# Two 2048-wide blocks on one core: query and key projection in paired 512-column steps, and three shifts in the slot tables around it

## What is computed

```python
hn = _rmsnorm(h, norm1_g)
q, k, v, u = jnp.split(hn @ w_in, [1024, 2048, 3072], axis=-1)
attn_out = dilated_attention(rope(q), rope(k), v)       # 8 heads of 128
bu = einsum('bsgp,gnp->bsgn', u, b_bar)                 # S5 input, 64 groups x 64 states, complex
_, states = lax.associative_scan(combine, (a_seq, bu))  # along the 256 tokens
y = einsum('bsgn,gpn->bsgp', states, c_mat).real + d_skip * u
```

## Time and profile before

| what | value |
|---|---|
| time, median of 3 runs | 3140.21 us (3140.12 to 3142.82) |
| the profiled execution | 3142.39 us, span 3140.7 us, granted clock 0.997 |
| PE busy | 3087.9 us, 98% of the span |
| DVE busy | 2036.6 us, 65% |
| ACT busy | 1632.1 us, 52% |
| POOL busy | 320.0 us, 10% |

### The profile page before, as it was taken

The page is one execution under the profiler, slowest core; times in us unless marked ns, Lnnn a source line. Parts: engine busy times, 40 slices in busy tenths (PEclk is TensorE's granted clock), DMA queues, the critical chain, the costliest instruction groups (busy, mean ns, idle before and its releaser), DMA issues.

```text
span 3140.7 us, 47334 instructions
## 1 busy us (share of the span) xinstructions
PE 3087.9 (98%) x17098; PEld 2691.0 (86%) x17098; DVE 2036.6 (65%) x2406; ACT 1632.1 (52%) x2088; POOL 320.0 (10%) x313
## 2 busy tenths in 40 slices
PE   8999999999999999999999999999999999999998
PEld 7989878888888888899998887888887888888887
DVE  7998987665566565657766777455555655555555
ACT  5545655654444365658754555445445544444453
POOL 1563440000000000004420000000000000000000
PEclk9999999999999999999999999999999999999999
DMA  8766666666666665555565555566655666666664
GB/s 296 247 224 186 193 184 197 188 189 190 193 187 187 201 188 167 193 185 171 177 189 187 175 165 177 184 195 209 200 184 158 200 191 191 191 189 192 193 188 154
DMA packets 176780, 600.99 MB, mean 191 GB/s; under 512 B 20320, under 2 KB 30688, under 8 KB 175488
## 3 DMA queue, kind: packets, MB, share of 16 engines
q1 hardware_dynamic: 164016, 567.18, 58.1%
q10 hardware_dynamic: 8976, 18.68, 1.6%
q0 software_dynamic: 3648, 13.24, 1.3%
HBM read 588.54 MB, written 10.49 MB: 191 GB/s over the span
## 4 chain that ended last, share of the span: by engine, by line
PE 84%; DVE 10%; issue 2%; ACT 1%; DMA 1%; POOL 1%; ACTq 0%; SPq 0%; DVEq 0%; POOLq 0%
PE gemm_psum L402 39%; PE gemm_psum L450 22%; PE gemm_psum L460 11%; PE gemm_psum L430 8%; DVE weights_lo L1471 3%; DVE late L1630 1%; PE gemm_psum L426 1%; DVE late L1623 1%; ACT weights_hi L876 1%; DVE late L1617 1%; DVE late L1634 1%; DVE late L1624 1%; DVE late L1633 0%; PE bank_s L737 0%; PE bank_s L705 0%
## 5 line engine op out<-in xcount | busy, mean ns | idle before, releaser
L1471 DVE TENSOR_TENSOR weights_lo<-weights,weights_hi 128x1024 fp32r<-128x1024 f32 (+1 forms) x1064 | 1312.4, 1238 | 896.6 <-ACT weights_hi L876 895.3
L876 ACT ACTIVATE weights_hi<-weights 128x1024 fp32r<-128x1024 f32 (+1 forms) x1064 | 1109.2, 1051 | 1113.1 <-PE gemm_psum L402 621.6
L450 PE MATMUL gemm_psum<-x_parts,weights_hi 128*128 128x512 f32 x3008 | 754.0, 392 | 0.7 <-DVE x_parts L2201 0.7
L450 PEld LDWEIGHTS gemm_psum<-x_parts,weights_hi 128*128 128x128 f32 x3008 | 541.6, 189 | 98.2 <-DVE x_parts L2201 0.9
L460 PEld LDWEIGHTS gemm_psum<-x_parts,weights_lo 128*128 128x128 f32 x3008 | 410.3, 190 | 29.3
L460 PE MATMUL gemm_psum<-x_parts,weights_lo 128*128 128x256 f32 x3008 | 419.4, 282 | 0.0
L402 PE MATMUL gemm_psum<-weights_hi,u_hi 128*128 128x512 f32 x1472 | 393.8, 389 | 0.0
L402 PE MATMUL gemm_psum<-weights_lo,u_hi 128*128 128x512 f32 x1472 | 387.4, 385 | 0.2 <-DVE weights_lo L1471 0.2
L402 PE MATMUL gemm_psum<-weights_hi,u_lo 128*128 128x512 f32 x1472 | 387.1, 385 | 0.0
L402 PE MATMUL gemm_psum<-weights_hi,x_parts 128*128 128x512 f32 x1280 | 322.9, 394 | 2.8 <-DVE x_parts L1682 1.9
L402 PEld LDWEIGHTS gemm_psum<-weights_lo,u_hi 128*128 128x128 f32 x1472 | 272.8, 188 | 56.6 <-DVE weights_lo L1471 0.9
(11 more groups left out here) (396 smaller groups left out, 2242.2 us busy)
## 6 DMA issues: line engine op xcount, KB each, us to landing
weights<-in_w_branch SPq DMA_DIRECT2D x192, 512.0 KB, 3.6
weights<-in_w_gu SPq DMA_DIRECT2D x176, 512.0 KB, 3.7
weights<-in_w_up SPq DMA_DIRECT2D x128, 512.0 KB, 4.2
weights<-in_w_down SPq DMA_DIRECT2D x128, 512.0 KB, 4.2
weights<-in_w_dn SPq DMA_DIRECT2D x64, 512.0 KB, 4.2
weights<-in_w_in_qk SPq DMA_DIRECT2D x32, 512.0 KB, 4.8
weights<-in_w_mem_k SPq DMA_DIRECT2D x32, 512.0 KB, 3.9
weights<-in_w_mem_v SPq DMA_DIRECT2D x32, 512.0 KB, 4.0
```

The source lines that it names most:

```text
L450: mm = pe.matmul(GP[:, 2 * p + n, :], HI[:, j % RING, cols], XS[:, (j % UNITS) * g.kt + k, :, :].rearrange("p a t -> p (a t)"), start=firs ...
L876: act.activation(HI[:, j % RING, 0:g.kt * GC], RAW[:, j % RING, 0:g.kt * GC], ACT.Copy)\
L1471: dve.tensor_tensor(LO[:, j % RING, cols], RAW[:, j % RING, cols], HI[:, j % RING, cols].bitcast(f32), ALU.subtract).then_inc(lo_done, 1)
```

## The change

There are four edits.

1. `in_qk` is run by `unit_pairs`. ACT gets a copy of the second halves in slots 3 and 7, and DVE's single multiply of the result by the row norm becomes an add, a wait for it, and a multiply in place.
2. In the first body of `in_qk`, the two `ssm_in` move from slots 2 and 4 to slots 4 and 6 on PE; on DVE the first `rotate_in` moves from slot 0 to 1 and the first scan from slot 2 to 3.
3. The scores of each head move on PE from slot 4 to slot 5.
4. In slot 6 of `mem_k` and `mem_v`, DVE runs the reciprocal before the scan instead of after it.

```diff
             def ssm(slot, b, q0):                              # PE
                 q, half = b.halved().plus(q0), b.c % 2
-                if slot == (2 if isinstance(b(), int) and b() == 0 and q0 == 0 else 0):
+                opening = isinstance(b(), int) and b() == 0 and q0 == 0
+                if slot == (4 if opening else 0):
                     ssm_in(q, 2 * half)
...
-                if slot == 4:
+                if slot == (6 if opening else 4):
                     ssm_in(q, 2 * half + 1)
...
-                if slot == 4:
+                if slot == 5:
                     wait(pe, rope_done, h(1, 1))
...
                     ssm(j, b, 0)
-                    units(in_qk, b, j, x)
+                    unit_pairs(in_qk, b, j, rows_before=False)
...
             def qk_events(slot, b):                            # ACT
                 ssm(slot, b, 0)
+                if slot in (3, 7):
+                    p = slot // 4
+                    wait(act, mm_done, b(SLOTS, SLOTS * in_qk.first + slot + 1))
+                    act.activation(ZP[:, ix(b(4, 8 + 2 * p), 2), :], GP[:, 2 * p:2 * p + 2, T:2 * T], ACT.Copy).then_inc(half_done, 1)
...
             def ssm(slot, b, q0):                              # DVE
                 s = b.times(2).plus(4 * q0)
-                if slot in (0, 4):
+                opening = isinstance(b(), int) and b() == 0 and q0 == 0
+                if slot in ((1, 4) if opening else (0, 4)):
                     rotate_in(s.plus(slot // 4), slot // 4)
-                if slot in (2, 6):
+                if slot in ((3, 6) if opening else (2, 6)):
                     scan_and_rotate_out(s.plus(slot // 4), slot // 4)
...
                 if slot in (3, 7):
-                    scaled_out(in_qk, b, slot, ZP[:, ix(b(4, 8 + 2 * (slot // 4)), 2), :])
+                    p = slot // 4
+                    tiles = ZP[:, ix(b(4, 8 + 2 * p), 2), :]
+                    wait(dve, half_done, b(2, p + 1))
+                    dve.tensor_tensor(tiles, GP[:, 2 * p:2 * p + 2, 0:T], tiles, ALU.add).then_inc(evac[p], 1)
+                    wait(dve, evac[p], b(1, in_qk.evacs + 1))
+                    dve.tensor_tensor(tiles, tiles, row(rms[:, 0, :]), ALU.mult)
...
             def mem_k_events(slot, b):
+                if slot == 6:
+                    attention(slot, b)
                 ssm(slot, b, 3)
-                attention(slot, b)
+                if slot != 6:
+                    attention(slot, b)
```

More of the change, by code:

```diff
@@ L1728, in mem_v_events @@
             def mem_v_events(slot, b):
+                if slot == 6:
+                    attention(slot, b.plus(4))
                 ssm(slot, b, 5)
-                attention(slot, b.plus(4))
+                if slot != 6:
+                    attention(slot, b.plus(4))
                 if slot in (3, 5) and b() > 0:
@@ L1828, in halves_added @@
                 p = slot // 4
-                wait(dve, half_done, b(2, halves + p + 1))
+                wait(dve, half_done, b(2, 2 * in_qk.bodies + halves + p + 1))
                 dve.tensor_tensor(dst, GP[:, 2 * p:2 * p + 2, 0:T], half, ALU.add).then_inc(evac[p], 1)
```

## The result

The changed kernel takes **3148.51 us** (median of 12 runs, 3146.72 to 3149.75), the kernel before 3141.43 (12 runs, 3139.55 to 3144.65). The ratio is 1.002, with a 95% interval of 1.0013 to 1.0028: about 7 us slower, where I had forecast 1.2.

The account below looks back on a forecast made before the run. DVE's list, with its ACT and POOL echoes, was taken to bound up to 443 us. +0.5 + 2.8 + 0.6 - 2.7 = +1.2 us took the median from 3140.2 to 3141.4; range 3133.5 to 3147.

Parts of the forecast that it names:

- What bounds: Up to 443 us DVE's list with its echoes (ACT and POOL waiting on DVE's work) bounds; PE is outside.
- Rival C: PE bounds after all, so its savings add up: 14.3 us, 3126, or half of it, 3133; chance 0.15.
- The reciprocal ahead of the scan: In `mem_v`, ACT's 0.82 wait and DVE's 0.81 go, four times, at most 3.2 us; 2.7 taken as gain.
- The multiply beside POOL: In slot 3 of `in_qk`, the new multiply runs beside POOL; price 0 to 8.3 us, 0.6 taken.
- Rival D: The new multiply in `in_qk` collides with POOL at the full price of 8.3: +8.9 us, 3149; chance 0.13.
- Six multiplies: Bodies 1 to 3 of `in_qk`: new DVE multiplies cost 4.2 us, less 1.4 of swallowed POOL waits: +2.8.
- The opening: Up to the third rotation: PE is freed by 7 us, DVE by nothing; third rotation at 100.9, +0.5 us.
- Paired steps on PE and the scores: PE saves 2.6 us in `in_qk` units and 4.6 of waits at the scores; both count 0.

Follow-up runs that it names:

- experiment 9: The kernel before with only ACT's eight stores of the `mem_k` results moved one slot later: 3133.22 us, 8.3 less than before.
- experiments 1: The kernel before with the paired steps alone, opening, scores and reciprocal as before: +5.4 us over the kernel before.
- 5: The changed kernel with the opening put back as before: +7.1 us over the kernel before, as the changed kernel.
- experiment 6: The changed kernel with a second pair of product buffers: +6.8 us over the kernel before; the same with the reciprocals behind the scan again: +5.4.
- `without_pairs`: The changed kernel with the paired steps undone; opening, scores and reciprocal stay moved: +0.8 us over the kernel before.
- experiment 10: `mem_k` stores one slot later in the changed kernel: 3139.82 us; in one without paired steps, ACT copying results, norm in the rope tables: 3131.97 us.

## Why the prediction was wrong

*What bounds.* Right for both kernels. DVE's list with its echoes sets the time up to 443 us. The stores moved in experiment 9 make the strongest case, since they touch only a wait of DVE and gave 8.3 us. Rival C fell with experiments 1, 5 and 9.

*The reciprocal ahead of the scan, -2.7.* This is the step that failed most: it measured **+0.5**, 3.2 us of the 4.9 by which the shift at `lower_out` was missed. The wait for ACT did go as forecast. What failed is the next step, that DVE's idle 0.81 becomes time won. POOL ran its last operation in that idle time, in 0.74. With the wait gone the `LO` starts before it, POOL's operation takes 1.70 to 1.74, and `rotate_in`, the next thing in DVE's list, waits 0.7 for it. The price stood in my own, 0.73 alone and 1.77 beside a `LO`; I used it for the new multiply and not for a `LO` that moves. From scan to `rotate_in` it takes 6.13 us where it took 6.09, and the 0.1 us of the reciprocal ahead of the scan is added in every body. No run moves the `LO` alone, so the collision is read from the traces (28 bodies with the edit against 16 without); that `rotate_in`'s wait for POOL holds the gain back is shown by experiment 6.

*The multiply beside POOL, +0.6.* Mis-sized. Over bodies 1 to 3 the collision measured 79.11 - 77.29 = 1.8 us, and 2.4 between the medians with the opening in it. It was within my bounds of 0 and 8.3, and I set it too low by the argument that DVE and POOL interleave there anyway. They do take turns, as the lines can be read, and the one that comes second waits for much of the rest of the other's operation. Rival D had the right mechanism, but its place is slot 3 only, as it said itself: the multiplies of slot 7 take 0.7. Together with the reciprocal's `LO`, this collision of DVE and POOL is behind most of the miss.

*Six multiplies, +2.8.* Right in size: 2.7 with the collision away. In part this is luck: I let 1.4 us of waits vanish, and 2.8 vanished, while DVE's list grew by 5.5 where I had 4.2.

*The opening, +0.5.* First rotation 72.04 (forecast 72.4), scan 81.73 (81.1), second rotation 87.28 (87.3). The last agreement is luck: the scan was 0.6 late, and the chain through POOL took 5.55 us, not the 6.2 of before, since `rotate_in` had no wait for POOL left there. The `LO` of unit 10 came at 94.67 (94.8), without a wait for weights. The third rotation came at 101.54 instead of 100.9. Before it stand four operations on the second input (L1700) that took 3.35 us together beside POOL, where they took 1.67 before. With the moved opening they take 2.9 to 3.4 in nine of ten kernels (1.94 in `without_pairs`), with the old one 1.7 to 1.8 in all four. The medians don't confirm that this costs time.

*Paired steps on PE and the scores, 0.* Right for the paired steps in all settings that were tried, and for the scores as long as the stores stand in their old place; behind the moved stores the scores may have a share in the 1.0 us of experiment 10.

*Sum.* 0.5 + 2.8 + 0.6 - 2.7 = 1.2 was forecast; 1.1 + 4.5 + 0.5 = 6.1 was measured at `lower_out`. The range ended at 3147.0, because I counted the full collision of the multiplies as the only way to be slower. Losing the one saving in the sum was another, and it had no rival of its own.

## What to carry to other kernels

Before a wait is booked as a gain, ask what the engine will do in the idle time that comes free, and what runs beside it there: another engine may have used that time, and the next wait may be for just that engine. An instruction moved "to an earlier slot" may have been put ahead of a longer chain. Where an engine that is ahead stands at a store or a DMA issue for a result that a slower engine makes, see what is queued behind it; here three `HI` stood there, and moving the store by one slot gave more than all four edits together took away.

## What the runs showed of the hardware

- The collision of DVE with POOL depends on where the operands lie, and both directions are seen. Beside POOL a multiply of 512 columns took 1.22 us with two SBUF inputs and 0.69 with one input from PSUM; in the second case POOL's next operation went from 1.06 to 1.68, beside a `LO` that began 0.01 ahead of it (110.25 against 110.26).
- Which of the two is drawn out goes, in these traces, by which begins first. In `mem_v`, a `LO` that began 0.24 us behind POOL's operation left it at 0.74; one that began 0.09 ahead drew it out to 1.74, with POOL's and DVE's instructions the same.
- PE's granted clock fell after two short stalls. In the changed kernel PE stood 2.08 us (until 80.61) and 1.91 us (until 87.41); the eight matmuls of 512 columns that began at 88.96 took 3.53 us instead of 2.00. Windows of that kernel (us, busy of PE, PEld, DVE, ACT, POOL, then the granted clock, DMA share and GB/s); 1.00 is 2.4 GHz, and 0.52 is nearly the level of 1.2 GHz:

```profile
83.00:88.00 5.00, 3.09 (x19) 2.41 (x18) 4.93 (x7) 2.12 (x2) 3.52 (x4) 1.00 1.04 365
88.90:92.40 3.50, 3.50 (x11) 2.73 (x11) 3.50 (x4) 1.80 (x4) 2.25 (x2) 0.52 1.00 412
```

  No cost of it is seen: from there to 450 us DVE never stands for PE.
- With a fixed order on each engine, a stretch bounded by DVE repeats to some 0.06 us from kernel to kernel, while single times of one kernel scatter over 2 to 5 us. Edits of 0.5 us can be priced by such a stretch, where the time alone can't.
